# Attention of the second block: the heads of group b first, no clock-keeping products between them, and the low halves of weights shared out anew

## What is computed

```python
proj = h @ w_in[l]                      # 256 x 1024 by 1024 x 1536: qa, ka, va, qb, kb, vb
qa = apply_axial_rope(rms_norm_2(qa, qn_g[l]), cos, sin)   # group a: 8 heads, normed, rotated
ka = apply_axial_rope(rms_norm_2(ka, kn_g[l]), cos, sin)
oa = global_attention(qa, ka, va)                          # softmax over all 256 keys
ob = window_sink_attention(qb, kb, vb, sink[l], slopes)    # group b: 8 heads, not rotated;
                                                           # distance slope, window, sink
mix = concatenate([rms_norm_2(oa), rms_norm_2(ob)]) @ w_o[l]
h = layer_norm(ALPHA * h + mix, ln1_g[l], ln1_b[l])
ffn = peer_ffn(h, wq[l], keys[l], u[l], v[l])   # top 16 x 8 of 16384 experts per token
h = layer_norm(ALPHA * h + ffn, ln2_g[l], ln2_b[l])
```

## Time and profile before

| | us |
|---|---|
| median of 3 runs (2640.53, 2633.37, 2639.18) | 2639.18 |
| time of the profiled execution | 2633.16 |
| its span | 2631.3 |
| PE busy | 2512.1 (95%) |
| DVE busy | 1767.3 (67%) |
| ACT busy | 1240.7 (47%) |
| POOL busy | 504.8 (19%) |

### The profile page before, as it was taken

The page is one execution under the profiler, slowest core; times in us unless marked ns, Lnnn a source line. Parts: engine busy times, 40 slices in busy tenths (PEclk is TensorE's granted clock), DMA queues, the critical chain, the costliest instruction groups (busy, mean ns, idle before and its releaser), DMA issues.

```text
span 2631.3 us, 43837 instructions
## 1 busy us (share of the span) xinstructions
PE 2512.1 (95%) x17391; PEld 2262.1 (86%) x17391; DVE 1767.3 (67%) x3113; ACT 1240.7 (47%) x2661; POOL 504.8 (19%) x387
## 2 busy tenths in 40 slices
PE   7898999999899999999999999799999999999997
PEld 6768897998679999999888887679999999888886
DVE  4647334445668975888777556668975888777556
ACT  5441134445345454444555555345454444555554
POOL 3600143544436600000000000536600000000000
PEclk9999799999899999999999999899999999999999
DMA  5400034664324566556678665314566655688664
GB/s 176 134 3 1 25 104 153 185 191 156 109 59 151 163 183 181 184 184 183 208 237 244 198 195 172 112 49 152 163 183 182 184 183 181 207 244 242 197 193 150
DMA packets 146027, 421.09 MB, mean 160 GB/s; under 512 B 15904, under 2 KB 49056, under 8 KB 145440
## 3 DMA queue, kind: packets, MB, share of 16 engines
q1 hardware_dynamic: 142032, 405.34, 50.8%
q0 software_dynamic: 2192, 8.99, 1.0%
q10 hardware_dynamic: 1600, 3.96, 0.4%
HBM read 400.40 MB, written 17.83 MB: 159 GB/s over the span
## 4 chain that ended last, share of the span: by engine, by line
PE 76%; DVE 16%; DMA 3%; ACT 2%; issue 1%; POOL 1%; DVEq 0%; ACTq 0%; SPq 0%
PE pb L418 75%; DMA raw<-in_vT 2%; PE pb L427 2%; DVE arena L2039 1%; DVE arena L2031 1%; DVE arena L2033 1%; DVE arena L2062 1%; DVE arena L2036 1%; DVE arena L2028 1%; DVE arena L1430 1%; DVE arena L1860 1%; ACT hi L1015 1%; DVE arena L1433 1%; DVE lo L1440 1%; DVE arena L1580 1%
## 5 line engine op out<-in xcount | busy, mean ns | idle before, releaser
L1015 ACT CAST hi<-raw 128x512 fp32r<-128x512 f32 x1402 | 815.3, 620 | 409.1 <-DMA raw<-in_vT 187.0
L418 PE MATMUL pb<-HTh,hi 128*128 128x256 f32 (+1 forms) x2968 | 860.6, 290 | 9.9 <-DVE lo L1440 9.9
L418 PE MATMUL pb<-HTl,hi 128*128 128x256 f32 (+1 forms) x2968 | 844.9, 285 | 0.0
L418 PE MATMUL pb<-HTh,lo 128*128 128x256 f32 (+1 forms) x2968 | 844.4, 284 | 0.0
L1440 DVE TENSOR_TENSOR lo<-raw,hi 128x1024 fp32r<-128x1024 f32 x476 | 579.9, 1220 | 92.4 <-ACT hi L1015 92.4
L2201 POOL TENSOR_TENSOR lo<-raw,hi 128x512 fp32r<-128x512 f32 x359 | 487.9, 1382 | 576.7 <-ACT hi L1015 576.2
L418 PEld LDWEIGHTS pb<-HTh,hi 128*128 128x128 f32 x2968 | 573.1, 193 | 12.4 <-issue 10.4
L418 PEld LDWEIGHTS pb<-HTl,hi 128*128 128x128 f32 x2968 | 573.5, 193 | 0.9
L418 PEld LDWEIGHTS pb<-HTh,lo 128*128 128x128 f32 x2968 | 572.5, 193 | 0.0
L418 PE MATMUL pb<-hi,WH 128*128 128x512 f32 x1112 | 434.5, 391 | 7.4 <-DVE WL L2165 7.4
L418 PE MATMUL pb<-lo,WH 128*128 128x512 f32 x1112 | 433.5, 390 | 0.0
(11 more groups left out here) (191 smaller groups left out, 2310.2 us busy)
## 6 DMA issues: line engine op xcount, KB each, us to landing
raw<-in_uT SPq DMA_DIRECT2D x256, 512.0 KB, 3.7
raw<-in_vT SPq DMA_DIRECT2D x256, 512.0 KB, 4.3
raw<-in_w_ffn_in SPq DMA_DIRECT2D x44, 512.0 KB, 3.6
raw<-in_wq SPq DMA_DIRECT2D x32, 512.0 KB, 3.7
wk<-kept SPq DMA_DIRECT2D x128, 128.0 KB, 4.3
raw<-in_w_in SPq DMA_DIRECT2D x24, 512.0 KB, 4.0
raw<-in_w_ffn_out SPq DMA_DIRECT2D x22, 512.0 KB, 4.3
raw<-in_w_gate SPq DMA_DIRECT2D x16, 512.0 KB, 3.5
```

The costliest lines, as they stand in the source:

```text
L418: return e.matmul(o, l, r, start=start, stop=stop)
L1015: e.copy(u.hi[k], u.half[k]).then_inc(*s.up("hi", ("hi", g)))
```

## The change

In both layers of the second block:

- The order of heads is turned: 8 to 15 (group b) first. `turn_tile` of 9, 5, 6 stands before the loop, 7 and 8 in its iterations 0 and 1, all copied to `QT` by ACT; tiles 0 to 4 are turned in iterations 3 to 7 and copied by DVE. The copies to `PT` are made by ACT for iterations 1 to 8 and by DVE after.
- The `warm` products in the loop and the 6 before it are left out.
- `low` is `dve` for units 4 to 11 of `win`, and `pool` for `u` 0 to 23 (was 0 to 17). `pick`, `gate_sums`, `gate_parts` and the turn of `SEL` stand 6 (the last two 4) units later.
- POOL applies gain and bias to `Hv`, and squares group b where it squared group a. Its DMAs for the gains of the next norm and the low part of the third unit of `wo` stand before that. ACT makes the high part of this unit in iteration 9.
- `wo` is taken in the order 4 to 7, 0 to 3.

```diff
+HEADS = list(range(8, 16)) + list(range(8))
+WO = (4, 5, 6, 7, 0, 1, 2, 3)
...
-                    low=both if (i, g) < (0, 2) else pool)
-        for c in range(8):
+                    low=dve if i else both if g < 2 else pool)
+        for c in WO:
...
-            add(("u", l, j), d["uT"][l, j], low=pool if j < 18 else dve)
+            add(("u", l, j), d["uT"][l, j], low=pool if j < 24 else dve)
...
-        project(2, 0, q_tiles)
-        turn_tile(4, ("ka", l))
-        warm(5, 6)
+        project(2, 0)
+        for f in (9, 5, 6):
+            turn_tile(f, ("qb", l))
...
-        for h in range(18):
-            if h < 16:
-                at_scores(h)
-            if h < 5:
-                turn_tile((9, 5, 6, 7, 8)[h], ("qb", l))
-            if 1 <= h <= 16:
-                at_turn(h - 1)
-                warm((h - 1) % 2, 5)
-            if h >= 2:
-                at_pv(h - 2)
+        for i in range(18):
+            if i < 16:
+                at_scores(i)
+            if i < 2:
+                turn_tile(7 + i, ("qb", l))
+            elif 3 <= i < 8:
+                turn_tile(i - 3, ("ka" if i == 7 else "qa", l))
+            if 1 <= i <= 16:
+                at_turn(i - 1)
+            if i >= 2:
+                at_pv(i - 2)
...
+            if n == 9:
+                split_high(units.i + 3)
...
-        for f in range(5):
-            turn_tile(f)
...
-            if h < 5:
-                turn_tile((9, 5, 6, 7, 8)[h])
-            if 1 <= h <= 8:
-                w.wait_ge(*s.to("pt_ps", l, h - 1))
-                e.tensor_copy(m.PT[(h - 1) % 3], PB[2 + (h - 1) % 2][:, :]).then_inc(*up("tiles", ("pt", l, h - 1)))
-            if 4 <= h <= 7:
-                gain_step(h - 4, ("in", l), m.BC2 if l else m.bc, 2 * l)
+            if 3 <= n < 8:
+                turn_tile(n - 3)
+            if 9 <= n <= 16:
+                w.wait_ge(*s.to("pt_ps", l, HEADS[n - 1]))
+                e.tensor_copy(m.PT[(n - 1) % 3], PB[2 + (n - 1) % 2][:, :]).then_inc(*up("tiles", ("pt", l, HEADS[n - 1])))
...
-            elif 18 <= j < 42 and j % 2 == 0:
+            elif 24 <= j < 48 and j % 2 == 0:
...
+        spread(2 * l + 1, m.bc1, d["ln1_g_2"][l], d["ln1_b_2"][l])
+        split_low(units.i + 3)
...
+            tt(m.Hv[:, t, :], m.Hv[:, t, :], bc[:, 0:1024], M).then_inc(*s.up("gains_pool", ("gain", ("in", l), t)))
...
+            tt(m.Hv[:, t, :], m.Hv[:, t, :], bc[:, 1024:2048], A).then_inc(*s.up("gains_pool", ("gained", ("in", l), t)))
...
+            tt(m.OS[:, t, 512:1024], m.O[:, t, 512:1024], m.O[:, t, 512:1024], M).then_inc(*s.up("head_squares", ("o_sq", l, 1, t)))
```

More of the change, by code:

```diff
@@ L901, in at_pv, with late @@
             x.then_inc(*s.up("score_ps", ("pv_ps", l, h)))
[L903 to L912 removed]
+        for i in range(18):
[9 more added lines that the diff above has]
+                at_pv(i - 2)
         for b in (4, 5, 6, 7):
             free[b] = [("o", l, b)]
[L915 to L922, removed]
+        turned(("ob", l), m.OS, lambda t, k: ("os", l, 1, 1), range(4, 8), 2)
+        def late(n):
+            if n == 4:
+                turned(("oa", l), m.OS, lambda t, k: ("os", l, 0, 1), range(4), 2)
+        rows_product(lambda n: units.take("wo", l, WO[n]), lambda n: m.pair(m.HT, ALL, WO[n], ALL), 8,
+                     lambda n: ("turn", ("oa" if n > 3 else "ob", l), WO[n]), OB, ("wo_ps", l), late)
         emptied_by(OB, ("pre", l, 0))
@@ L1325, in at_scores @@
                     x.then_inc(*s.up("soft", *([("snk", l, h)] if t else [])))
[L1327 to L1330, removed]
-                w.wait_ge(*s.to("pt_ps", l, h - 1))
[L1332 to L1336, removed]
-        turned(("oa", l), range(4), 2, f"gn{l}")
[L1338 to L1344, removed]
+        for f in (9, 5, 6):
+            tile(f)
+        for n in range(18):
+            if n < 2:
+                tile(7 + n)
+            if n < 16:
+                at_scores(n)
+            if 1 <= n <= 8:
+                w.wait_ge(*s.to("pt_ps", l, HEADS[n - 1]))
+                if n > 3:
+                    w.wait_ge(*s.to("pv_ps", l, HEADS[n - 4]))
+                e.copy(m.PT[(n - 1) % 3], PB[2 + (n - 1) % 2][:, :]).then_inc(*s.up("soft", ("pt", l, HEADS[n - 1])))
+            if n == 9:
+                split_high(units.i + 3)
+            if n == 15:
+                w.wait_ge(*s.to("o_ms", l, 1))
+                fn(m.s16[:, :, 8:16], m.v16[:, :, 8:16], ACT.Sqrt).then_inc(*s.up("roots", ("o_root", l, 1)))
+        turned(("ob", l), range(4, 8), 2, f"gn{l}")
+        take("wo", l, 4)
+        w.wait_ge(*s.to("o_ms", l, 0))
+        fn(m.s16[:, :, 0:8], m.v16[:, :, 0:8], ACT.Sqrt).then_inc(*s.up("roots", ("o_root", l, 0)))
+        for c in range(5, 8):
+            take("wo", l, c)
+        turned(("oa", l), range(4), 2, f"gn{l}")
+        for c in range(4):
             take("wo", l, c)
@@ L1997, in vector @@
[L1997 to L2003, removed]
-                head_mean(1, 1)
-                head_root(1)
-                head_norm(1, 0)
-                head_norm(1, 1)
-            if c == 4:
-                turned(("ob", l), range(4, 8), 2, f"gn{l}")
-            take("wo", l, c)
+        for n in range(18):
+            if n < 16:
+                at_scores(n)
+            if 3 <= n < 8:
+                turn_tile(n - 3)
+            if 9 <= n <= 16:
+                w.wait_ge(*s.to("pt_ps", l, HEADS[n - 1]))
+                e.tensor_copy(m.PT[(n - 1) % 3], PB[2 + (n - 1) % 2][:, :]).then_inc(*up("tiles", ("pt", l, HEADS[n - 1])))
+            if n == 10:
+                over(1)
+            elif n in (11, 12):
+                values(1, n - 11)
+            elif n in (13, 14):
+                head_mean(1, n - 13)
+            elif n == 15:
+                head_root(1)
+            elif n > 15:
+                head_norm(1, n - 16)
@@ L2012, in residual @@
+        turned(("ob", l), range(4, 8), 2, f"gn{l}")
+        for n in range(8):
+            if n == 1:
+                over(0)
+                values(0, 0)
+                values(0, 1)
+                head_mean(0, 0)
+                head_mean(0, 1)
+                head_root(0)
+                head_norm(0, 0)
+                head_norm(0, 1)
+            if n == 4:
+                turned(("oa", l), range(4), 2, f"gn{l}")
+            take("wo", l, WO[n])
         def residual(dst, name, banks, out, tag):
```

80 lines of the change are left out of this document (37 added, 43 removed).

## The result

| | before | changed |
|---|---|---|
| median, us | 2636.27 (4 runs, 2632.92 to 2640.53) | 2659.49 (4 runs, 2658.05 to 2662.21) |
| profiled execution, us | 2633.16 | 2658.05 |
| its span, us | 2631.3 | 2656.2 |
| ratio to before | 1 | 1.0088 (95% interval 1.0068 to 1.0109) |

The change made the kernel slower by 23 us. The direction and the mechanism were as forecast, and the time lies in the range, but the size was half of what the sum said: 2683 stood for a loss of 44, or 47 against the median of before with its fourth run.

A forecast was written before the change was run, and what follows sets the result against it. PE was taken as the bound. Per layer, start of scores, heads, work behind them and experts (-6.5 + 32.0 + 3.9 - 6.8; -9.5 + 34.4 + 3.0 - 6.6) gave +43.9 on 2633.16, 2677, plus 6.0: 2683 us, range 2642 to 2704.

The forecast's parts named there:

- the start of the scores: From first projection product to first scores: 43.0 us for 49.5 and 52.5 before, a gain of 6.5 and 9.5 us.
- the way from the first scores to the last transposes: Head loop of each layer: 86.4 us for 54.4 and 52.0 before, a loss of 32.0 and 34.4 us.
- The clock in the heads: PE's clock falls to 0.50 in the heads' first idle times and stays there until the product with `wo`.
- Rival 1: Clock comes back to full in group a, about 11 us less a layer and 3 behind: 2655 us; chance 0.15.
- The bank wait: Iterations 3 to 7: transposes wait for DVE's copy of the q tile; 4.8 us an iteration at 1.00, for 3.1.
- Rival 4: Bank wait in the heads does not bite, 4 x 5 us less with the clock low: 2650 us; chance 0.06.
- Behind the heads, and `u`: After the heads to the end of `wo`: loss of 3.9 and 3.0 us; experts' `u`: gain of 6.8 and 6.6.
- From the trace to the median: Sum on the profiled 2633.16 us gave 2677; 6.0 us added because the median of the runs is higher: 2683.
- Rival 2: Clock holds at 1.00 all along, head loop 54 us plus 3 to 4 for POOL's stall: faster, 2618 us; chance 0.13.
- Rival 3: POOL and DVE collide at group b's sinks, or POOL falls behind in `u` 18 to 23: 2696 us; chance 0.09.
- POOL's operations on `Hv`: Four operations in the heads, 8 to 11 us, hidden at half clock; at full clock DVE would stall some 3 us.

The follow-up runs named there:

- experiment two: Changed kernel with the five late q tiles turned into the other bank, still no bf16 products: 2638.53 us, ratio 1.0026 to the kernel before.
- experiment six: Kernel before, in its old order and banks, with the bf16 products in and ahead of the head loop left out: 2672.41 us, ratio 1.0153.
- experiment seven: Changed kernel with the low parts of the input projection made by POOL again: 2667.57 us, ratio 1.0128 to the kernel before.
- Experiment five: Kernel before with only the experts' part of the change (`u` 0 to 23 on POOL, steps of `SEL` later): 2618.44 us, ratio 0.9937.
- experiment four: Changed kernel with five late tiles in the other bank, bf16 products back, 20 more ahead of the loop's first transposes: 2595.27 us, ratio 0.9861; again 2595.11.
- experiment nine: The kernel of experiment four without the bf16 products in the iterations from 9 on (heads of group a): 2603.13 us, ratio 0.9889 to the kernel before.
- experiment three: Changed kernel with the bf16 products back and the five late tiles in the other bank: 2601.25 us, ratio 0.9876 to the kernel before.
- the first (758.84): Changed kernel with the bf16 products back (5 in each iteration, 6 ahead of the loop), bank wait left: 2645.54 us, ratio 1.0049 to the kernel before.

## Why the prediction was wrong, point by point

The mechanism was right and the sum was off: it said +43.9 us between the two traces and they are 24.9 apart. Two terms of the sum failed, the start of the scores (7.2 us over both layers) and the way from the first scores to the last transposes (6.9). Another 4.6 us lie in `v`, where no difference was forecast, and 4.6 more came from the step from the traces to the medians.

- **The clock in the heads**: right in both halves. It fell behind the first wait (696.5) and did not come back until the product with `wo` (788.7), through 32.40 gapless us of group a. Experiments two and six show it without the bank wait, in the new and in the old order of heads. Rival 1, by which a busy PE would be back at full clock in group a, did not come true.
- **The bank wait**: right in its place, all five stand there, each 1.61 us in front of the transposes and released by DVE's copy of the tile. Rival 4 is out, and its price of 33 us was too large as well: experiment two took the wait away and gained 16. The 4.8 us of an iteration at full clock adds up to 4.7 from its own parts, and no run had the waits at full clock.
- **First scores to last transposes**: the mechanism was right and a term too large. Values were put at 2.0 us at half clock, twice the 1.0 at full clock, with 1.75 and 2.5 as bounds; scores and values together take 3.81, so the values are 1.8. That makes 6.95 for 7.1 five times and 4.65 for 4.9 eight times, 2.8 us; the first transposes came 0.3 earlier, and the last step was 0.4 shorter. Together 3.5 us a layer.
- **The start of the scores**: the term that failed most. The rotation's four operations were priced at 1.87 from the earlier trace rows, a row that lies beside POOL's subtractions, although the text said that POOL would stand idle. They take 0.89 then, and experiment seven turned them back into 5.18 and 2.98. Two rotations make 1.9 of the 2.6 us by which DVE's steps were shorter from the squares on; the squares began 0.5 later than forecast, and the last low part ended at 684.98, 34.0 after the first product, where 36.0 was forecast. PE then did not wait for this low part but for the one before it, for 1.10 us (and 1.02 before that) where two waits of 2.5 were forecast, and ended at 37.2 for 38.8. From there to the first scores it was 2.5 us, not the 4.2 of the sum: 1.2 of that sum stood for a fall of the clock, which stayed at 1.00 until 696.5, and ACT's copies held PE up for 0.72 for 1.1, as one half of them ran beside PE's last products. So 3.3 and 3.9 us too little gain.
- **Behind the heads, and `u`**: right within 0.2 us in all four terms. Experiment five confirms `u` by itself, and with it that POOL keeps pace.
- **What was not in the sum**: `v` of layer one took 3.9 us less. In the trace of before PE waited 2.46 us in it for a weight that came late, and fell to half clock; in the changed one the same wait was 1.72 and the clock held. The rows, first of before and then of the changed kernel:

```profile
1588.41 0.76 PE L418 MATMUL pb<-hi,WH 128*128 128x512 f32 x1 [2.46 <-DVE WL L2165]
```

```profile
1601.30 0.47 PE L421 MATMUL pb<-hi,WH 128*128 128x512 f32 x1 [1.72 <-DVE WL L2174]
```

  The change doesn't touch this stage. It took 353.0 to 355.2 us in the three traces with the old attention part and 350.0 to 354.1 in the eleven with the new one; the two ranges overlap, so it looks like scatter that happened to lie in the profiled execution on which the sum was built. That is not shown.
- **From the trace to the median**: 6.0 us were added because the profiled execution of before was that much below its median. With one more run it was 3.1 below, and the changed kernel's was 1.4 below. That is 4.6 us of the miss.
- **Rival 2** (the clock holds, faster): not this kernel, but experiment four made its condition true, with 2595 where the rival gave 2618 for a loop that still had the bank wait.
- **Rival 3** (POOL and DVE collide): they did, and it cost nothing here. The addition of the sinks took 1.68 us beside POOL's operations on `Hv` (751.34) and PE had no gap in group a. In `u` POOL did not fall behind.
- **POOL's operations on `Hv`**: the four took 9.3 us, within the 8 to 11, and were hidden at half clock as forecast. At full clock they cost PE a wait (1.02 us in the fourth kernel's first layer, 2.10 in experiment nine); the prediction had 3 us for it.

## What to carry to other kernels

When filler products are taken out, price the clock and not the products: here 0.55 us of products a head held up a clock worth 1.6. Two causes that each hold the clock down hide each other, so an experiment that takes away only one tells little; take away both. And a duration is a price only together with what ran beside it: read from the same row's moment what the other engines did.

## What the runs showed of the hardware

- Which work brings TensorE's clock back was unlike which work holds it. Float32 scores, transposes and values, without a gap, stayed at 0.50 for 32.40 us (changed kernel) and 37.50 us (experiment six). The same work, started at 1.00, stayed at 1.00 for the 14 us of experiment nine's first layer. With five bf16 products a head the clock came back to 1.00 within 7 us in experiment three (697.4 to 704.2), but in the kernel before only at 714.4, 16 us after the first transposes. The float32 products of 512 columns with `wo` brought it back as well (782.80 to 788.7 in the changed kernel), so the type alone does not decide it; which property of the bf16 products did was not tried.
- In the head loops of the traces every fall of the clock came in a wait of PE of 0.98 us or more, or at most 2.2 us behind one. Not every such wait brought a fall: 0.98 passed in one layer of experiment nine and not in the other, 1.02 passed twice in the fourth kernel, and 1.51 once in the first (758.84).
- POOL at work made DVE operations with two inputs in SBUF 2 to 6 times longer: 0.89 to 1.87, 2.98 and 5.18 for the same four, 0.29 to 1.18 and 1.27 for two of k's in the changed kernel (685.11 and 686.32) beside the subtractions of `wo`. It is not only two inputs: a DVE operation on 128x2 numbers with one input took 2.18 us for 0.17 beside POOL's operations on `Hv`, in the fourth kernel:

```profile
735.67 4.66 POOL L2265 TENSOR_TENSOR H<-H,arena 128x1024 f32<-128x1024 f32 x2
735.87 2.18 DVE L1445 TENSOR_SCALAR arena<-arena 128x2 f32<-128x2 f32 x1
...
740.19 0.17 DVE L1445 TENSOR_SCALAR arena<-arena 128x2 f32<-128x2 f32 x1
```

  DVE's operations that read a product bank kept their lengths there (0.68 and 0.69 for 128x512). The traces show what the length goes by: each of the short slow operations ended within 0.15 us behind the POOL operation that was running. The one above ended at 738.05, and the first of POOL's two at 738.02. The 1.18 and 1.27 ended at 686.29 and 687.59, POOL's subtractions at 686.14 and 687.44; the 1.68 of the sinks ended at 753.02, POOL's operation at 752.99. The square of 7.35 us in the earlier trace rows lasted through six subtractions that followed each other without a gap (1652.93 to 1660.43) and ended 0.56 us behind them; when DVE gets in between two of them and when it does not stays open.
